# The experts' input weights read as two runs a partition, the token rows kept without a stride

## The chip, the cores and the metric

One NeuronCore of a Trainium2 chip runs the whole program in one launch. The metric is device time in microseconds (us), from one profiled execution and from runs without a profile; lower is better. All arithmetic is float32.

## The reference

Two transformer blocks in a row over 256 tokens of width 1024. The first block (two layers) mixes a convolution, a latent attention and a dilated attention. The second block has an attention over tokens and context and then a mixture of experts, cut here to what matters:

```python
logits = xt @ w_router + b_router
top_val, top_idx = lax.top_k(logits, 4)          # 4 of 32 experts a token
gates = softmax(top_val)
# for each expert e, its rows xb (tokens that chose it):
hcat = xb @ w_in[e] + b_in[e]                    # w_in[e] is 1024 x 2048
x_glu = minimum(hcat[:, :1024], 7)
x_lin = clip(hcat[:, 1024:], -7, 7)
act = x_glu * sigmoid(1.702 * x_glu) * (x_lin + 1)
y += gate * (act @ w_out[e] + b_out[e])          # w_out[e] is 1024 x 1024
```

An expert's weights are 8 MiB + 4 MiB, and all 32 experts are read once: 384 MiB of the 563 MB that the program moves.

## The kernel before

The kernel is written engine by engine. Each engine runs its own hand-ordered program, and semaphores join them: SyncE (SP) issues the DMA loads, TensorE (PE) multiplies and transposes, ScalarE (ACT) and VectorE (DVE) take results out of PSUM.

**Weights of the experts.** `ring` is an SBUF tensor of six tiles, each 128 partitions x 4096 float32 (2 MiB). An expert fills all six: tiles 0 to 3 hold w_in (256 of its 1024 rows each), tiles 4 and 5 hold w_out. `expert_tile` issues one DMA for one tile and counts it on `mlanded[j]`. Expert 0's tiles are asked for while the attention still runs. `expert(e, m)` then asks for the six tiles of the next expert, each as soon as PE has used the tile that lies there (`mused`, `lin_done`, `eout_done`); SP runs it in a loop over experts 1 to 31.

**Which row of w_in lies where.** A contraction over 1024 features is done in 8 steps of 128. Step 2j + r takes `xs[:, 2j + r, :]` (the expert's tokens, features on the partitions) and `ring[:, j, ...]`, the half r of tile j. For a given step it doesn't matter which feature sits on which partition, as long as both operands agree. Before, partition p of tile j holds rows 8p + 2j and 8p + 2j + 1, which are neighbours in HBM: one run of 16 KB a partition, with 64 KB from one partition's run to the next.

**Token rows.** After the norm the tokens lie as `h` (feature 128k + a on partition a, chunk k). PE turns them with `pe.transpose` into the PSUM bank `flip`, four chunks at a time (L830), and ACT copies each `flip` into `hTM`, tokens on the partitions (L1064). There are four such rounds, and PE waits for the copy (`flip_free`) before it turns the next four. `xs` is made per expert by `gather` (L858), which multiplies 128 columns of `hTM` at a time with a selection matrix, into `flip` and `score`; ACT copies these to `xs` (L1074). The copy of L1064 reads `flip` in a strided way, so that columns 128k to 128k + 127 of `hTM` are the features 8p + k, which is the order of the weights' rows.

**The path to the experts.** Router logits (L819), top 4 (L1297 on), the four copies, the exponential of the gates (L1068, behind the four copies in ACT's order), the gates on DVE (L1306 to L1314), their transpose (L843), the experts' output bias (L851), the first gather (L858), `xs` (L1074), and the first product of expert 0 (L869).

Of the kernel before, what the change touches and what calls it, by code (L numbers as in the profile page):

```python
# [21 lines left out]
ACT = mybir.ActivationFunctionType  # L22
AX = mybir.AxisListType

P = 128
# [3 lines left out]
DC = D // P  # L29
LAYERS = 2  # L30
EPS = 1e-6
W = 512
HALF = 64
# [186 lines left out]
def build(nc, c_in, xT, ctxT, consts, layer_params, block_params, w_in, w_uq, w_ukv, w_out_a, w_out_b, w_out_c,  # L220
          w_o, w_ada, w_qkv, w_o2, e_in, eb_in, e_out, eb_out, out, sizes=None, debug=None):
    PER = sizes or CHAINED
    with ExitStack() as ctx:
        def sb(name, shape, dt=F32):
            return ctx.enter_context(nc.sbuf_tensor(name, shape, dt))

        def sem(name):
            return ctx.enter_context(nc.semaphore(name))
# [12 lines left out]
        ring = sb("ring", [P, MRING, TILE])  # L241
# [29 lines left out]
        def take(*shape):  # L271
            n = 1
            for s in shape:
                n *= s
            v = space[:, top[0]:top[0] + n]
            top[0] += n
            if len(shape) == 2:
                return v.rearrange("p (a b) -> p a b", b=shape[1])
            if len(shape) == 3:
                return v.rearrange("p (a b c) -> p a b c", b=shape[1], c=shape[2])  # L280
            return v
# [71 lines left out]
        hTM = take(TT, D)  # L353
# [54 lines left out]
        flip = ctx.enter_context(nc.psum_tensor("flip", [P, W], F32))  # L408
# [26 lines left out]
        flip_free = sem("flip_free")  # L435
# [44 lines left out]
        mlanded = [sem(f"mlanded{i}") for i in range(MRING)]  # L480
# [35 lines left out]
        def done(l, u):  # L516

            return (l + 1) * NU + u + 1

        def split_count(l, k):  # L520

            return (l + 1) * NQ + k + 1
# [29 lines left out]
        def bdone(u):  # L552
            return (LAYERS + 1) * NU + u + 1
# [21 lines left out]
        def block_sync(sp):  # L575

            sp.wait_ge(mixed_free, MIXED0 + 1)
            sp.dma_start(bpar, block_params).then_inc(bpar_loaded, 16)
            sp.dma_start(ctx_x, ctxT).then_inc(bpar_loaded, 16)
            sources = [(w_qkv, 0, W), (w_qkv, W, 256), (w_qkv, 768, W), (w_qkv, 1280, W), (w_qkv, 1792, W)]  # L580
            sources += [(w_ada, (LAYERS * 4 + n) * W, W) for n in range(4)]
            sources += [(w_o2, 0, W), (w_o2, W, W)]
            for n, (src, a, width) in enumerate(sources):
                if n >= RING:
                    last = max(u for u, x_ in enumerate(BUNITS) if x_[1] == n - RING)
                    sp.wait_ge(unit_done, bdone(last))
                else:

                    if n < LRING:
                        sp.wait_ge(lo_done, split_count(LAYERS - 1, NQ - 1))  # L590
                    else:
                        sp.wait_ge(unit_done, done(LAYERS - 1, NU - 1))
                sp.dma_start(ring[:, n % RING, :].rearrange("p (c n) -> p c n", c=DC)[:, :, 0:width],
                             columns(src, a, width)).then_inc(landed[n % RING], 16)

            def expert_tile(we, wo, j):

                if j < 4:
                    src = we.rearrange("(p j r) n -> p j (r n)", p=P, j=4)[:, j, :]
                else:  # L600
                    src = wo.rearrange("(b p a) n -> p b (a n)", p=P, b=2)[:, j - 4, :]
                sp.dma_start(ring[:, j, :], src).then_inc(mlanded[j], 16)

            def expert(e, m):
                we = e_in[bass.ds(e, 1)].rearrange("a k n -> (a k) n")
                wo = e_out[bass.ds(e, 1)].rearrange("a k n -> (a k) n")
                for j in range(MRING):
                    if j == 3:
                        sp.wait_ge(lin_done, m)
                    elif j == 5:  # L610
                        sp.wait_ge(eout_done, m)
                    else:
                        sp.wait_ge(mused, m * 4 + (0, 1, 2, 3, 3)[j] + 1)
                    sp.sem_inc(asked, 1)
                    expert_tile(we, wo, j)

            assert (len(sources) - 2) % RING == 1
            for j in (4, 5, 3, 0, 1, 2):  # L620
                if j in (0, 3):
                    sp.wait_ge(unit_done, bdone(BQKV - 1))
                elif j in (1, 2):
                    sp.wait_ge(unit_done, bdone(NBU - 1))
                expert_tile(e_in[0], e_out[0], j)
            sp.wait_ge(mix_ready, 1)
            sp.dma_start(bout[0:NEXP, :], eb_out).then_inc(bpar_loaded, 16)
            sp.wait_ge(table_ready, 1)
            sp.dma_start(bin_sb[0:NEXP, :], eb_in).then_inc(bpar_loaded, 16)
            with sp.Fori(1, NEXP) as e:  # L630
                expert(e, e)
            sp.wait_ge(table_ready, 2)
            n_jobs = sp.value_load(jobi[0:1, MAXJOBS:MAXJOBS + 1], min_val=0, max_val=MAXJOBS)
            with sp.If(n_jobs > 0):
                with sp.Fori(0, n_jobs) as i:
                    e = sp.value_load(jobi[0:1, bass.ds(i, 1)], min_val=0, max_val=NEXP - 1)
                    expert(e, i + NEXP)
            for i in range(DC // 2):
                sp.wait_ge(final_ready, i + 1)
                sp.dma_start(out[:, 2 * i:2 * i + 2, :], h[:, 2 * i:2 * i + 2, :]).then_inc(stored, 16)  # L640
            sp.wait_ge(stored, 16 * (DC // 2))
# [341 lines left out]
        def block_scalar(act):  # L983
# [77 lines left out]
            for r in range(4):  # L1061
                t, q = r // 2, r % 2
                act.wait_ge(flipped, FLIP0 + F_TOK + r + 1)
                act.activation(hTM[:, t, :].rearrange("p (k a) -> p a k", k=DC)[:, q * HALF:(q + 1) * HALF, :],  # L1064
                               flip[:, :].rearrange("p (a k) -> p a k", k=DC), ACT.Copy).then_inc(flip_free, 1)
            act.wait_ge(gate_in, 1)
            for t in range(TT):
                ins = act.activation(gate[:, t, :], ext[:, t, 0:NEXP], ACT.Exp, bias=gsum[:, t, 0:1])  # L1068
# [376 lines left out]
        def columns(weights, a, n):  # L1445
            return weights[:, a:a + n].rearrange("(c p) n -> p c n", p=P)
# [298 lines left out]
        def _(act):  # L1745
# [214 lines left out]
            if debug != "layers":  # L1960
                block_scalar(act)
# [416 lines left out]
```

## Time and profile before

| | |
|---|---|
| median of 3 runs | 2039.31 us (2038.09 to 2044.0) |
| the profiled execution, its own time | 2037.97 us |
| its span, first to last instruction | 2036.2 us |
| mean granted TensorE clock | 0.981 |
| PE busy | 1904.2 us (94%) |
| DVE busy | 759.7 us (37%) |
| ACT busy | 546.9 us (27%) |
| DMA packets | 111407, 563.19 MB |
| in_e_in loads | 128 of 2048 KB, median 25.2 us from issue to landing |
| in_e_out loads | 64 of 2048 KB, median 22.1 us |

PE busy counts a matmul as busy while it waits in the array's pipeline, so a high share doesn't say that PE is the limit. The experts' stage is the second half of the span, from 1089 us on. The time from issue to landing of a load holds its wait behind earlier loads in the DMA queue.

### The profile page before, as it was taken

The page shows a single profiled execution, that of the slowest core. Times are in us where ns is not written, and L with a number is a line of the kernel's source. Part 1 is how long each engine was busy: PE and PEld are TensorE (multiplying, and loading weights), DVE is VectorE, ACT ScalarE, POOL GpSimd, SP SyncE. Part 2 cuts the span into 40 slices and gives each one's busy share as a digit, 9 for nine tenths or more (in the row PEclk, how much of TensorE's full clock was granted, in tenths as well). Part 3 has the DMA queues.
Part 4 walks back from the last instruction along what each step waited for, and adds up shares of the span by engine and source line. Part 5 has one row for each costly group of instructions (what it writes and reads, how often), then busy time and mean ns, then how long its engine had stood idle before and what let it go on. Part 6 is the DMA issues. An engine that isn't in the chain of part 4 may idle for free.

```text
span 2036.2 us, 26901 instructions
## 1 busy us (share of the span) xinstructions
PE 1904.2 (94%) x10970; PEld 1199.2 (59%) x10970; DVE 759.7 (37%) x1445; ACT 546.9 (27%) x922; POOL 522.6 (26%) x220
## 2 busy tenths in 40 slices
PE   7999999989999999799879999999999999999996
PEld 6779889977798899544465444333333333333433
DVE  4784643448836533734544111111111111111112
ACT  4554455445544554222411000000000000000001
POOL 5776656866755567000000000000000000000000
PEclk9999999999999999899998999999999999999999
DMA  8555333565543335421725999999999999999994
GB/s 297 200 183 176 125 125 125 172 231 176 201 150 130 120 125 189 158 75 42 287 93 208 430 428 428 430 428 429 428 428 429 428 428 429 429 429 428 428 429 193
DMA packets 111407, 563.19 MB, mean 277 GB/s; under 512 B 4768, under 2 KB 24352, under 8 KB 86464
## 3 DMA queue, kind: packets, MB, share of 16 engines
q1 hardware_dynamic: 111328, 562.09, 69.1%
q8 instruction: 56, 0.92, 0.2%
q14 instruction: 23, 0.19, 0.0%
HBM read 561.02 MB, written 1.05 MB: 276 GB/s over the span
## 4 chain that ended last, share of the span: by engine, by line
PE 57%; DMA 31%; DVE 7%; ACT 2%; issue 1%; SPq 0%; DVEq 0%; ACTq 0%
DMA ring<-in_e_in_dram 31%; PE bank L1595 14%; PE bank L1585 10%; PE score L869 9%; PE bank L695 4%; PE bank L1562 3%; PE mixed L904 2%; PE bank L802 1%; PE mixed L1679 1%; PE flip L1662 1%; DVE ring L2164 1%; PE score L1648 1%; PE flip L1620 1%; PE bank L927 1%; PE score L887 1%
## 5 line engine op out<-in xcount | busy, mean ns | idle before, releaser
L1971 POOL TENSOR_TENSOR w_lo<-ring,w_hi 128x1024 fp32r<-128x1024 f32 (+1 forms) x216 | 522.4, 2430 | 285.2 <-ACT w_hi L1873 284.6
L869 PE MATMUL score<-ring,space 128*64 128x512 f32 x2048 | 461.4, 595 | 46.2 <-DMA ring<-in_e_in_dram 45.2
L869 PEld LDWEIGHTS score<-ring,space 128*64 128x64 f32 x2048 | 142.3, 137 | 353.9 <-issue 246.2
L1873 ACT ACTIVATE w_hi<-ring 128x1024 fp32r<-128x1024 f32 (+1 forms) x216 | 226.3, 1049 | 221.5 <-PE bank L1595 122.5
L1595 PE MATMUL bank<-h_hi,w_hi 128*128 128x256 f32 x896 | 261.9, 292 | 0.0
L1595 PE MATMUL bank<-h_lo,w_hi 128*128 128x256 f32 x896 | 254.3, 284 | 0.0
L1595 PE MATMUL bank<-h_hi,w_lo 128*128 128x256 f32 x896 | 254.2, 284 | 0.0
L904 PE MATMUL mixed<-ring,space 128*64 128x512 f32 x1024 | 226.8, 595 | 0.0
L1083 ACT ACTIVATE space<-space 128x512 f32<-128x512 f32 x32 | 20.2, 631 | 718.9 <-DVE space L1375 718.9
L1375 DVE TENSOR_SCALAR space<-score 128x512 f32<-128x512 f32 x32 | 22.2, 694 | 431.7 <-PE score L869 431.7
L1595 PEld LDWEIGHTS bank<-h_hi,w_hi 128*128 128x128 f32 x896 | 172.8, 193 | 4.5 <-issue 4.4
L1595 PEld LDWEIGHTS bank<-h_lo,w_hi 128*128 128x128 f32 x896 | 172.7, 193 | 0.1
L1595 PEld LDWEIGHTS bank<-h_hi,w_lo 128*128 128x128 f32 x896 | 172.4, 192 | 0.0
L904 PEld LDWEIGHTS mixed<-ring,space 128*64 128x64 f32 x1024 | 70.7, 137 | 132.6 <-issue 130.6
L1585 PE MATMUL bank<-w_hi,h_hi 128*128 128x512 f32 (+1 forms) x320 | 131.4, 411 | 8.3 <-DVE h_lo L2027 8.3
L1388 DVE COPY space<-mixed 64x512 f32<-64x512 f32 x32 | 21.9, 685 | 295.6 <-PE mixed L904 295.6
L1585 PE MATMUL bank<-w_hi,h_lo 128*128 128x512 f32 (+1 forms) x320 | 124.9, 390 | 0.0
L1585 PE MATMUL bank<-w_lo,h_hi 128*128 128x512 f32 (+1 forms) x320 | 124.6, 389 | 0.0
L1585 PEld LDWEIGHTS bank<-w_hi,h_hi 128*128 128x128 f32 x320 | 61.0, 191 | 25.6 <-issue 12.5
L695 PE MATMUL bank<-ring,h 128*128 128x512 f32 (+1 forms) x160 | 66.6, 569 | 5.1 <-DVE h L1148 5.1
L1585 PEld LDWEIGHTS bank<-w_lo,h_hi 128*128 128x128 f32 x320 | 61.2, 191 | 11.7 <-issue 1.0
L1585 PEld LDWEIGHTS bank<-w_hi,h_lo 128*128 128x128 f32 x320 | 60.9, 190 | 12.0
(320 smaller groups left out, 2330.7 us busy)
## 6 DMA issues: line engine op xcount, KB each, us to landing
ring<-in_e_in_dram SPq DMA_DIRECT2D x128, 2048.0 KB, 25.2
ring<-in_e_out_dram SPq DMA_DIRECT2D x64, 2048.0 KB, 22.1
ring<-in_w_in_dram SPq DMA_DIRECT2D x42, 2048.0 KB, 7.8
ring<-in_w_ada_dram SPq DMA_DIRECT2D x16, 1024.0 KB, 5.4
ring<-in_w_o_dram SPq DMA_DIRECT2D x6, 2048.0 KB, 7.9
ring<-in_w_qkv_dram SPq DMA_DIRECT2D x4, 2048.0 KB, 9.9
ring<-in_w_ada_dram SPq DMA_DIRECT2D x4, 2048.0 KB, 8.0
ring<-in_w_out_a_dram SPq DMA_DIRECT2D x2, 2048.0 KB, 7.7
```

The lines of the kernel that those rows point to most:

```text
L695: ins = pe.matmul(b[:, 0:n], src[:, c, tt * P:(tt + 1) * P], w8[:, c, 0:n], start=c == 0, stop=c == DC - 1)
L802: ins = pe.matmul(b[:, i * T:(i + 1) * T], w8[:, c, m:m + P], mix[:, c, :], start=c == 0 and i == 0, stop=c == DC - 1, skip_group_check=True)
L869: ins = pe.matmul(score[HALF * blk:HALF * blk + HALF, which * W:(which + 1) * W], xs[:, 2 * j + r, HALF * hh:HALF * hh + HALF], wk[:, blk ...
L887: pe.matmul(score[HALF * blk:HALF * blk + HALF, which * W:(which + 1) * W], onehot[:, hh, :], bin_sb[:, at:at + W], start=False, stop=False)
L904: ins = pe.matmul(mixed[HALF * side:HALF * side + HALF, :], actT[:, hh, a * P + HALF * half:a * P + HALF * half + HALF], ring[:, 4 + half, ...
L1375: dve.tensor_scalar(glu[:, hh, :], score[:, 0:W], GLU_LIMIT, None, ALU.min).then_inc(glu_free, 1)
L1388: dve.tensor_copy(ys[0:HALF, hh, :], mixed[0:HALF, :])
L1562: ins = pe.matmul(b[:, i * T:(i + 1) * T], w_[:, c, m], y_[br][:, c, :], start=c == 0 and i == 0 and y_ is y_hi and w_ is hi, stop=c == 3 ...
L1585: ins = pe.matmul(b[:, 0:n], x_[:, c, t], w_[:, k % PARTS, i, 0:n], start=c == 0 and x_ is h_hi and w_ is w_hi, stop=c == DC - 1 and x_ is ...
L1595: ins = pe.matmul(b[:, half * T:(half + 1) * T], w_[:, k % PARTS, i, m:m + P], x_[:, c, :], start=c == 0 and half == 0 and x_ is h_hi and ...
L1873: act.activation(split_part(w_hi, k), raw_part(k), ACT.Copy).then_inc(hi_done, 1)
L1971: pool.tensor_tensor(split_part(w_lo, k), raw_part(k), split_part(w_hi, k), ALU.subtract).then_inc(lo_done, 1)
```

## The change

`expert_tile` reads w_in in another order: partition p of tile j now holds rows 256j + p and 256j + 128 + p, which lie 128 rows (1 MB) apart in HBM. A partition's 16 KB are two runs of 8 KB, and the tile as a whole is one contiguous 2 MiB region. Tiles 4 and 5 (w_out) are as before. Since step 2j + r now takes the features 128 (2j + r) + p, `hTM` keeps the order in which PE turns the tokens, and the copy from `flip` has no stride.

```diff
             def expert_tile(we, wo, j):
                 if j < 4:
-                    src = we.rearrange("(p j r) n -> p j (r n)", p=P, j=4)[:, j, :]
+                    src = we.rearrange("(j r p) n -> p j r n", p=P, j=4)[:, j, :, :]
+                    dst = ring[:, j, :].rearrange("p (r n) -> p r n", r=2)
                 else:
                     src = wo.rearrange("(b p a) n -> p b (a n)", p=P, b=2)[:, j - 4, :]
-                sp.dma_start(ring[:, j, :], src).then_inc(mlanded[j], 16)
+                    dst = ring[:, j, :]
+                sp.dma_start(dst, src).then_inc(mlanded[j], 16)
...
             for r in range(4):
                 t, q = r // 2, r % 2
                 act.wait_ge(flipped, FLIP0 + F_TOK + r + 1)
-                act.activation(hTM[:, t, :].rearrange("p (k a) -> p a k", k=DC)[:, q * HALF:(q + 1) * HALF, :],
-                               flip[:, :].rearrange("p (a k) -> p a k", k=DC), ACT.Copy).then_inc(flip_free, 1)
+                act.activation(hTM[:, t, q * W:(q + 1) * W], flip[:, :], ACT.Copy).then_inc(flip_free, 1)
```

SP's program, in the loop over the experts (`ISA` is the count on `asked`, `REGISTER_ALU` the loop's counters). Before:

```order
65 L602 ISA [waits mused]
66 L602 DMA ring<-in_e_in_dram 128x4096
67 L613 REGISTER_ALU
68 L602 ISA [waits mused]
69 L602 DMA ring<-in_e_in_dram 128x4096
...
76 L602 ISA [waits mused]
77 L602 DMA ring<-in_e_out_dram 128x4096
```

and now:

```order
65 L604 ISA [waits mused]
66 L604 DMA ring<-in_e_in_dram 128x2x2048
67 L615 REGISTER_ALU
68 L604 ISA [waits mused]
69 L604 DMA ring<-in_e_in_dram 128x2x2048
...
76 L604 ISA [waits mused]
77 L604 DMA ring<-in_e_out_dram 128x4096
```

Nothing moved in SP's program; the four w_in loads of an expert have a pattern of 128 x 2 runs of 2048 elements, and the w_out loads have the one that they had.

ACT's program, at the four copies of the token rows (`space` is the SBUF tensor in which `hTM`, `gate` and `xs` lie). Before:

```order
683 L1064 ACTIVATE space<-flip 128x64x8 [waits flipped] x4
684 L1068 ACT_TABLE_LOAD
685 L1068 ACTIVATE space<-space 128x32 [waits gate_in]
686 L1068 ACTIVATE space<-space 128x32
687 L1074 ACTIVATE space<-flip 128x512 [waits gathered_half]
688 L1074 ACTIVATE space<-score 128x512 [waits gathered_half]
```

and now:

```order
683 L1066 ACTIVATE space<-flip 128x512 [waits flipped] x4
684 L1069 ACT_TABLE_LOAD
685 L1069 ACTIVATE space<-space 128x32 [waits gate_in]
686 L1069 ACTIVATE space<-space 128x32
687 L1075 ACTIVATE space<-flip 128x512 [waits gathered_half]
688 L1075 ACTIVATE space<-score 128x512 [waits gathered_half]
```

The four copies stand where they stood; their pattern is now that of the later copies from `flip`. No engine has an instruction more or fewer.

## Rows read from the trace of the kernel before

**Rows 1.** The page, the span in 40 slices of 50.9 us: DMA share in tenths, GB/s.

```profile
DMA  8555333565543335421725999999999999999994
GB/s 297 200 183 176 125 125 125 172 231 176 201 150 130 120 125 189 158 75 42 287 93 208 430 428 428 430 428 429 428 428 429 428 428 429 429 429 428 428 429 193
```

**Rows 2.** The chain of waits (start us, us, what), pieces of the experts' stage.

```profile
1109.16 7.02 PE mixed L904 x32
1136.37 7.02 PE mixed L904 x32
...
1267.57 25.42 DMA ring<-in_e_in_dram
1292.99 0.04 issue
1293.04 3.68 PE score L869 x16
1296.72 0.02 issue
...
1972.39 25.43 DMA ring<-in_e_in_dram
```

**Rows 3.** Windows: us, busy us by engine, TensorE clock, DMA share, GB/s.

```profile
1122.00:1270.00 148.00, 147.31 (x735) 62.70 (x732) 28.77 (x64) 11.57 (x19) 0.00 (x0) 1.00 1.01 429
1270.00:1564.00 294.00, 274.80 (x1345) 112.83 (x1344) 50.62 (x111) 21.28 (x35) 0.00 (x0) 1.00 1.01 429
1858.00:2005.00 147.00, 137.19 (x675) 56.18 (x674) 24.26 (x50) 11.41 (x19) 0.00 (x0) 1.00 1.01 429
```

**Rows 4.** Windows of 3 and 2 us in which loads run; columns as before.

```profile
662.00:665.00 3.00, 3.00 (x27) 2.83 (x28) 0.92 (x4) 2.65 (x5) 0.00 (x0) 1.00 1.06 410
801.00:803.00 2.00, 2.00 (x19) 2.00 (x18) 0.69 (x1) 1.06 (x1) 2.00 (x1) 1.00 1.04 429
```

**Rows 5.** DMA view of 745 to 770 us, 40 slices: two loads of 4 KB rows.

```profile
GB/s 0 0 0 0 0 0 131 151 295 419 426 419 419 419 419 269 0 13 0 0 0 0 0 0 0 0 0 0 0 66 105 203 387 413 413 419 419 419 406 98
```

**Rows 6.** DMA view of 1122 to 2005 us.

```profile
DMA packets 25971, 378.33 MB, mean 428 GB/s; under 512 B 2880, under 2 KB 2880, under 8 KB 2880
q1 hardware_dynamic: 25970, 378.32, 100.6%
```

**Rows 7.** DMA view of 1304.9 to 1309.8 us, about one tile.

```profile
DMA packets 144, 2.10 MB, mean 428 GB/s; under 512 B 16, under 2 KB 16, under 8 KB 16
```

**Rows 8.** Timeline around the four copies (start us, us, engine line).

```profile
1062.72 1.03 ACT L1064 ACTIVATE space<-flip 128x512 f32<-128x512 f32 x1 [11.15 <-PE flip L830]
1063.81 0.66 PE L830 MATMUL flip<-cst,h 128*128 128x128 f32 x4 [1.12 <-ACT space L1064]
1068.64 1.04 ACT L1064 ACTIVATE space<-flip 128x512 f32<-128x512 f32 x1 [1.21 <-PE flip L830]
1069.69 1.28 ACT L1068 ACT_TABLE_LOAD   x1
1071.56 0.23 DVE L1306 TENSOR_TENSOR space<-space 128x64 f32<-128x64 f32 x1 [7.35 <-ACT space L1068]
1088.93 7.09 PE L869 MATMUL score<-ring,space 128*64 128x512 f32 x32 [0.98 <-ACT space L1074]
```

**Rows 9.** Source view of L1064 and of L1074: ns min/median/max.

```profile
L1064 ACT ACTIVATE space<-flip x4: 1030/1032/1039, 1062.7 to 1068.6; 128x512 f32<-128x512 f32 x4
L1074 ACT ACTIVATE space<-flip x17: 598/598/598, 1085.8 to 2003.5; 128x512 f32<-128x512 f32 x17
```

**Rows 10.** Windows ahead of the experts' stage; columns as before.

```profile
1067.00:1074.00 7.00, 3.85 (x18) 3.49 (x18) 1.56 (x8) 3.29 (x5) 0.00 (x0) 0.50 0.00 0
1074.00:1082.00 8.00, 7.42 (x19) 5.17 (x17) 7.24 (x26) 0.00 (x0) 0.00 (x0) 0.50 0.01 2
1082.00:1089.00 7.00, 6.01 (x35) 5.83 (x36) 6.51 (x9) 1.20 (x2) 0.00 (x0) 0.68 0.00 0
```

**Rows 11.** Window with the last of expert 0's input tiles in the queue; columns as before.

```profile
1048.00:1055.00 7.00, 0.06 (x1) 0.00 (x0) 6.11 (x11) 0.42 (x1) 0.00 (x0) 0.81 1.03 442
```

## The prediction

> **What bounds the kernel now.** I read the slices of the page first. From the 23rd slice on the DMA engines are at 9 tenths and the rate stands at 428 to 430 GB/s, while before that it changes from slice to slice [rows 1]. So the second half of the span runs at a rate that something fixes. The windows say the same more finely: from 1122 to 2005 us the DMA share is 1.01 at 429 GB/s, while PE has room from 1270 us on (274.80 busy of 294) [rows 3]. In the chain of waits the reader is to see two regimes. Early on PE's own work follows itself: one expert's output product starts at 1109.16 us and the next one's at 1136.37, so PE needs 27.2 us an expert. From 1267.57 us the chain is a DMA wait of 25.4 us, 3.68 us of PE, and the next DMA wait [rows 2]. The pieces at 1267.57 and at 1972.39 us are 24 experts apart: 704.82 / 24 = 29.37 us an expert, or 4.895 us for each of its six 2 MiB tiles. The 25.4 us are not the price of one load: they are the queue, five tiles deep. DMA needs 29.37 us an expert and PE 27.2. The first 6 experts are paid out of the tiles that were loaded ahead, and from there the end of the program is the end of the DMA stream plus a tail.
>
> Two things follow. What a tile costs on the DMA engines counts in full from the first request of the loop (expert 1's) to the last tile, also where PE seems to be the limit, since the stream never stands still in between. And what PE, ACT or DVE do inside the stage counts for nothing, as long as PE stays under 29.37. Ahead of the stage, the start of the stream counts: the first request of the loop waits until PE has used expert 0's first tile, at the end of a chain of small steps [rows 8].
>
> **Part 1: the four copies.** L1064 takes 1.032 us. The copy from the same bank, of the same 128x512 elements with no stride, takes 0.598 us (L1074) [rows 9]. The changed line has that form, so I take 0.60 for it: 4 x 0.433 = 1.73 us less. All four are on the path. PE waits 1.12 us with its next four transposes until the copy before is done, and the fourth copy stands in ACT's order ahead of the table load and the exponential, for which DVE has been waiting 7.35 us; from there the chain goes on to the first product of expert 0 at 1088.93 us [rows 8]. Next in line behind the copies are PE's counting products, which stand behind the last transposes on PE and move up with them by three copies; they were done about 1 us before DVE came to their result, so they don't take the place of the copies.
>
> Some of the 1.73 us may be given back by the clock. In this stretch PE is granted 0.50, its lower level of 1.2 GHz; PE begins to be busy without long pauses at about 1074.9 us, and the clock is back at full within the window that ends at 1089 (0.68 in the mean) [rows 10]. 0.68 over 7 us is 2.5 us at full speed. If the return comes at the same moment as before, the 1.73 us of matmuls that ran in that time at 2.4 GHz now run ahead of it at 1.2 GHz and take twice as long, so that 0.87 us of the gain is left. I take the middle of 0.87 and 1.73, **-1.3 us**.
>
> **Part 2: the loads.** Each w_in tile was 128 runs of 16 KB, 8 an engine, and is now 256 runs of 8 KB, 16 an engine. A tile's window holds 144 packets, 128 of 16 KB and 16 small ones that close the load [rows 7]. The bytes are the same, so the question is what 8 more packets cost an engine. 31 experts pass the loop (expert 0's tiles come before it and lie landed for some 30 us before PE asks for them, which covers theirs): 31 x 4 x 8 = 992 more packets on each engine, one after another in a stream that never pauses.
>
> The trace of before has no saturated stream of 8 KB packets, so I bound the price from the other sizes.
> - 2 KB packets: with loads of 2 KB rows running, the rate is 410 GB/s (the first of [rows 4]). A tile would take 2.097 MB / 410 = 5.115 us, 0.220 us more than 4.895, with 64 packets an engine in place of 8. 0.220 / 56 = 3.9 ns a packet.
> - 4 KB packets: six slices in the middle of a load run at 419 (once 426), 420 in the mean [rows 5]. A tile would take 4.993 us, 0.098 more for 24 more packets: 4.1 ns a packet.
> - 8 KB packets: in the 2 us of a 1 MB load of such rows the rate is 429 (the second of [rows 4]), that of the 16 KB stream. By this the price is nothing. But the window is short against the 16 packets of 0.3 us that it cuts at each end, so it is a weak row; it is the lower end.
> - By the packets' own durations instead of the rate: 3 us x 16 engines x 1.06 over 1.23 MB / 2048 B = 600 packets is 84.8 ns for one of 2 KB [rows 4]. One of 16 KB is at most 883 us x 16 x 1.006 / 23,090 = 615.5 ns (25,970 less 2880 small ones) [rows 6]. (8 x 84.8 - 615.5) / 7 = 9.0 ns a packet. This is the upper end. It counts the overlap of a packet with the next one as cost, which the share of 1.06 shows to be there (over 1.00 can't be throughput), so I trust it less than the rates.
>
> I take 4.0 ns, since two sizes agree on it and 8 KB lies between one of them and the 16 KB that I measure from: 992 x 4.0 = **+4.0 us**, with 0 and 992 x 9.0 = +8.9 us as ends. An expert becomes 29.37 + 4 x 8 x 0.004 = 29.50 us. PE stays 2.3 us under it, so no part of it is hidden. SP issues as many DMAs as before, each about 20 us ahead of its turn in the queue; a longer issue would be covered by that queue, and only if the queue were empty would it show, once a tile.
>
> The Trainium skill weighs in here with another view of the limit: *DMA: Bandwidth & Descriptors*, section "Where 436 GB/s comes from", holds that for loads from HBM the HBM side binds, at about 358 GB/s a core, and not the port side (435). If that were the limit, a packet's overhead in the engine would be hidden behind HBM, part 2 would be nothing and the sum would be -1.3 us. The trace disagrees with 358: the stream holds 428 (the page itself allows more when the other core is idle).
>
> **Sum.** -1.3 + 4.0 = +2.7 us on the profiled execution's own 2037.97 us (1.8 us more than its span of 2036.2) gives 2040.7. The median of the runs shown, 2039.31, is 1.3 us above the profiled execution; on it the forecast is **2042.0 us**, +0.13%.
>
> **Rivals.** Differences under 0.3%, 6.1 us, are about what a measurement of this kernel can't tell from no change.
> 1. Slower: a packet costs what its duration says, 9.0 ns. Then +8.9 - 1.3 = +7.6, 2046.9 us. It decides from (6.1 + 1.3) / 992 = 7.5 ns a packet. For it speaks that durations are what the engines themselves record; against it that two rates at two sizes give half of it. A variant is that the jump of 1 MB between the two halves of a partition costs HBM something; loads of 2 KB rows jump at every packet and yet fit 4 ns. Chance 0.16.
> 2. The packets are free, as the 429 row would have it: -1.3 us, 2038.0 us. Chance 0.13.
> 3. Faster: the old pattern is what holds the stream at 428, since one partition's run is 64 KB from the next, and the contiguous tile runs quicker. The best rate that a longer window shows is 442 GB/s, over 7 us in which the last tiles of expert 0 come in [rows 11]. A w_in tile at 442 takes 4.745 us, 0.150 less: 124 x 0.150 = 18.6 us, and with part 1 the time is 2019.4 us. Against it: that 442 is itself from tiles of the old pattern; and w_out tiles are contiguous already, yet a third of the stream being such tiles leaves no trace, the rate standing at 428 to 430 in every slice [rows 1] and at 428 in the window of a single tile [rows 7]. It would decide from 6.1 - 1.3 = 4.8 us, 0.039 us a tile. Chance 0.05. A rule stands beside it: the Trainium skill's *DMA: Bandwidth & Descriptors*, "Latency and other measured facts", warns of row pitches at large powers of two in HBM, with measured losses from 512 KiB on, and advises to lay tiles out contiguously. By that rule the old 64 KB pitch is the suspect one and the change repairs it; no row here shows a loss at 64 KB.
>
> The forecast itself (a packet at 1 to 7 ns) has 0.62, and 0.04 is for something unseen, such as a clock that returns later ahead of the stage or at the tail.
>
> **How the numbers follow.** Within 0.3% are the forecast and rival 2, and half of the unseen: 0.77. Slower is rival 1 with a little of the unseen: 0.17. Faster: 0.06. The ends of the sum are -1.7 + 0 and -0.9 + 8.9, which on the median is 2037.6 to 2047.3. The runs of before spread over 6 us, with two of three within 1.2, so I widen the lower end by 1.6 and hold the upper: 2036 to 2047.5.
>
> **What the changed profile would show.** Right: packets rise by 128 x 128 = 16384 to some 127,790, with the count under 8 KB unchanged. An expert's period in the chain is 29.50 us (29.37 if the packets are free, 29.66 at 9 ns), and the stream's rate about 426.5 GB/s at a share above 1.00. The copies (now L1066) take 0.60 us and the first product of expert 0 starts at 1087.2 to 1088.1 us. Clock around it: still 0.50 from about 1066 us. Wrong: a period below 29.3 would be rival 3; a DMA share below 1 in the stage would mean that another part, such as issue by SP or the making of descriptors, limits the stream; and PE waiting elsewhere than on in_e_in tiles would mean that the change moved the wait.

## The result, and the profile after

The changed kernel takes 2046.56 us in the median of 14 runs (2044.14 to 2051.76); the kernel before, on the same chips, 2038.14 (2036.64 to 2044.0). The ratio is 1.0039, interval 1.003 to 1.0048: slower by 0.4%, some 8 us. The profiled executions differ by 7.1 us in their spans (2036.2 and 2043.3).

The page of the changed kernel: its DMA share and rate in 40 slices, the packets, and the queue's share of 16 engines.

```profile
DMA  8555333565544235411726999999999999999994
GB/s 296 201 183 174 125 124 124 178 232 178 193 145 146 103 136 194 161 53 42 288 90 256 425 423 424 425 422 425 424 425 423 424 425 423 423 425 425 422 425 193
DMA packets 127791, 563.19 MB, mean 276 GB/s; under 512 B 4768, under 2 KB 24352, under 8 KB 86464
q1 hardware_dynamic: 127712, 562.09, 69.5%
```

The same bytes come in 127,791 packets, 16,384 more. In the experts' stage the rate is 422 to 425 GB/s where it was 428 to 430 [rows 1], and the DMA share is as full as before (1.01 in the window below). The first half of the span is much as it was.

The chain of waits of the changed kernel, from the first product of expert 0 to the last wait for a w_in tile:

```profile
1086.69 7.09 PE score L871 x32
...
1266.92 25.73 DMA ring<-in_e_in_dram
...
1979.11 25.75 DMA ring<-in_e_in_dram
2004.86 0.04 issue
```

1266.92 and 1979.11 are 24 experts apart: 29.675 us an expert, where it was 29.37 [rows 2]. Laid out by the chains, the 7.1 us are: the first product of expert 0 2.24 us earlier (1086.69 for 1088.93, [rows 8]); from there to the landing of the last w_in tile 918.17 us for 908.89 (the wait of 25.43 us from 1972.39 ends at 1997.82), so 9.28 more; and from that landing to the end 38.44 for 38.38. The sum is +7.1.

Windows of the changed kernel, columns as in [rows 3], one of the stage and one ahead of it:

```profile
1270.00:1564.00 294.00, 271.78 (x1327) 110.12 (x1326) 48.43 (x104) 21.26 (x35) 0.00 (x0) 1.00 1.01 424
```

```profile
1082.00:1089.00 7.00, 5.99 (x39) 4.40 (x40) 5.66 (x10) 1.20 (x2) 0.00 (x0) 0.90 0.00 0
```

In the stage PE has more room than before (271.78 busy of 294, for 274.80), so DMA is still the slower one. Ahead of it the granted clock of 1082 to 1089 us is 0.90 in the mean, for 0.68 [rows 10]. The copies, source view:

```profile
L1066 ACT ACTIVATE space<-flip x4: 598/598/599, 1063.1 to 1067.6; 128x512 f32<-128x512 f32 x4
```

598 ns each, for 1032 [rows 9].

### The profile page after: what moved, and what is told of

It reads as the page before. It is cut to its first block, busy times and chain, and to the rows that moved or that the text cites. A ratio compares the mean times of both kernels' runs of the same rounds, so it can differ in the third digit from the quotient of the medians.

```text
span 2043.3 us, 26901 instructions
## 1 busy us (share of the span) xinstructions
PE 1904.1 (93%) x10970; PEld 1198.6 (59%) x10970; DVE 759.8 (37%) x1445; ACT 545.1 (27%) x922; POOL 522.4 (26%) x220
## 2 busy tenths in 40 slices
DMA packets 127791, 563.19 MB, mean 276 GB/s; under 512 B 4768, under 2 KB 24352, under 8 KB 86464
## 3 DMA queue, kind: packets, MB, share of 16 engines
HBM read 561.02 MB, written 1.05 MB: 275 GB/s over the span
## 4 chain that ended last, share of the span: by engine, by line
PE 56%; DMA 33%; DVE 7%; ACT 2%; issue 1%; SPq 0%; DVEq 0%; ACTq 0%
DMA ring<-in_e_in_dram 33%; PE bank L1596 14%; PE bank L1586 10%; PE score L871 9%; PE bank L697 4%; PE bank L1563 3%; PE mixed L906 2%; PE bank L804 1%; PE mixed L1680 1%; PE flip L1663 1%; DVE ring L2165 1%; PE score L1649 1%; PE flip L1621 1%; PE bank L929 1%; PE score L1693 1%
```

## The experiments

Two theories for the 0.307 us that an expert costs more. **A**: the count of packets, 32 more an engine and expert, each at 9.6 ns. **B**: only 4 ns of that is the count's, as the prediction took it, and the rest is the tile's new place in HBM, a contiguous region read with jumps of 1 MB. A has its 9.6 ns from this result, so it takes other kernels to test it. A period below is the distance of two waits in the chain, divided by the experts between them. "Before" beside a time is the kernel before on the same chip.

### The count or the place

**Runs of 8 KB in the old 64 KB block** (e1_runs8_near).

```diff
-src = we.rearrange("(j r p) n -> p j r n", p=P, j=4)[:, j, :, :]
+src = we.rearrange("(p r j) n -> p j r n", p=P, j=4)[:, j, :, :]
...
```

The copies of the token rows, left out here, are strided again, to fit this order of rows.

> The w_in tiles keep the old place in HBM (each partition its own block of 64 KB), but a partition's 16 KB are two runs of 8 KB, 32 KB apart (rows 8p + j and 8p + 4 + j). Theory A (the count of packets alone costs, 9.6 ns for each more on an engine): the period of an expert in the chain is 29.67 us as in the changed kernel. Theory B (only some 4 ns a packet are the count's, and the rest comes from the new place: a contiguous tile read with jumps of 1 MB): 29.50 us. The token copies are here 8 strided ones of 128x256, so the first product of expert 0 may start later than in both kernels, by either theory.

Its chain:

```profile
1267.87 25.73 DMA ring<-in_e_in_dram
...
1979.95 25.75 DMA ring<-in_e_in_dram
```

712.08 / 24 = 29.67 us. The place is the old one and the period the new one: theory B fell. One run took 2047.28 us (before 2038.77).

**A contiguous tile in runs of 16 KB** (e2_contig16, and again as e11_contig16_again).

```diff
-src = we.rearrange("(p j r) n -> p j (r n)", p=P, j=4)[:, j, :]
+src = we.rearrange("(j p r) n -> p j (r n)", p=P, j=4)[:, j, :]
...
-hTM[:, t, (4 * q + i) * P:(4 * q + i + 1) * P],
+hTM[:, t, (2 * q + i // 2) * 2 * P + i % 2:(2 * q + i // 2 + 1) * 2 * P:2],
```

The copies are the ones without a stride.

> The w_in tiles are contiguous 2 MiB regions as in the changed kernel, but a partition holds two neighbouring rows, one run of 16 KB (rows 256j + 2p and 256j + 2p + 1). The copies of the token rows have no stride; the gather reads every second column as PE's stationary operand. Theory A: 29.37 us an expert, as before the change, and with the cheaper copies some 2 us less than before, 2036. Theory B: between 29.37 and 29.67, about 29.5, since the tile's place is the new one. If a stationary operand with a stride is slow to load, PE's gathers get longer; PE has 2.2 us of room an expert, and two gathers of 16 products ahead of the stage lie on the path.

> The kernel with contiguous tiles in 16 KB runs and copies without a stride again, beside the two above: 29.37 us an expert and a ratio of 0.9988, 2.5 us under the kernel before, as far as five rounds can tell.

The chain, and the gather in the source view (ns min/median/max):

```profile
1292.98 25.43 DMA ring<-in_e_in_dram
...
1968.38 25.42 DMA ring<-in_e_in_dram
```

```profile
L858 PEld LDWEIGHTS flip<-space x272: 192/197/331, 1078.4 to 1999.2; 128*128 128x128 f32 x136
```

675.40 / 23 = 29.37 us, the period of before, from the contiguous place: A once more, from the other side. Loading every second column as stationary operand (the one loaded into PE ahead of a product) takes 197 ns in the median, against 191 in both kernels. The times are 2034.98 us (before 2038.77; ratio 0.999, 0.9979 to 1.0) and 2038.22 (before 2037.87; 0.9996, 0.9987 to 1.0005). One of the 12 runs behind the second time took 4524.81 us, and the ratio leaves it out; the median without it is 2037.9, and why it was so long is not known. So this layout has the changed kernel's copies without its packets, is 0.4 to 0.5% faster than the changed kernel by the two ratios, and against the kernel before can't be told from no change. The profiled span of e2_contig16, 2030.7 us, is 5.5 us under that of before, but only 2.5 us of that lie between L823 and expert 0's first product (25.0 us for 27.5); another 1.5 are the sums of the last norm at the end of the program (L980), with 3.73 us for 5.26, in which the next kernel and the changed one differ as well. Most of the rest lies ahead of L823.

**w_out in runs of 8 KB too** (e4_wout8).

```diff
-src = wo.rearrange("(b p a) n -> p b (a n)", p=P, b=2)[:, j - 4, :]
-dst = ring[:, j, :]
+src = wo.rearrange("(b s p a) n -> p b s (a n)", p=P, b=2, s=2)[:, j - 4, :, :]
+dst = ring[:, j, :].rearrange("p (s n) -> p s n", s=2)
...
-lin[:, hh, a::4]
+lin[:, hh, 256 * (a // 2) + a % 2:256 * (a // 2 + 1):2]
```

> The changed kernel with its w_out tiles too in two runs of 8 KB (rows 128 pairs apart), so 16 more packets an engine and expert. Theory A: 29.67 + 16 x 0.0096 = 29.83 us an expert, 4.8 us more in all than the changed kernel. Theory B (place of w_in): the w_out tiles add only 16 x 0.004 = 0.07 us, 29.74. If something else in the alternation of the two packet sizes costs the extra, the period stays at 29.67 or falls.

```profile
1267.18 25.87 DMA ring<-in_e_in_dram
...
1983.17 25.89 DMA ring<-in_e_in_dram
```

715.99 / 24 = 29.83 us, as A had it. The one time, 2047.69 us (before 2038.77), is less than the 4.8 us over the changed kernel that a longer stream should give, but the chain shows the whole of it: from expert 0's first product (1085.91 us) to the last landing of a w_in tile (1983.17 + 25.89 = 2009.06) it is 923.15 us, 5.0 more than the changed kernel's 918.17. What is missing is in the tail, where the 16 products that sum up the last norm are quicker; here those of the changed kernel first, then this kernel's:

```profile
2029.04 5.33 PE score L982 x16
```

```profile
2033.24 3.73 PE score L982 x16
```

Around them the granted clock is 0.69 in the mean in the changed kernel (2029.0 to 2034.4 us) and 1.00 in this one (2033.2 to 2037.0). In the kernel before they take 5.26 us.

### What a packet costs, from 2 KB to 32 KB

**Runs of 4 KB and of 2 KB** (e6_runs4, e7_runs2), the changed kernel with each w_in row in pieces:

```diff
-src = we.rearrange("(j r p) n -> p j r n", p=P, j=4)[:, j, :, :]
-dst = ring[:, j, :].rearrange("p (r n) -> p r n", r=2)
+src = we.rearrange("(j r p) (w n) -> p j w r n", p=P, j=4, w=2)[:, j, :, :, :]
+dst = ring[:, j, :].rearrange("p (w r n) -> p w r n", w=2, r=2)
...
```

This is the 4 KB kernel; the 2 KB kernel has `w=4`. The products, left out here, take the pieces from where they now lie in the tile.

> The changed kernel with each w_in row in two halves, so a tile is 512 packets of 4 KB, 32 an engine. Theory A in the form that the queued stream of the four kernels so far gives it (a packet lasts 9.3 ns plus its bytes at 27.2 bytes a ns, so 159.8 ns): 5.12 us a tile, 30.26 us an expert. By the prediction's 4 ns a packet, from loads that run alone: 4.99 us a tile, 29.76 us an expert.

> The same with rows in four quarters: a tile is 1024 packets of 2 KB, 64 an engine. Fixed price in the queued stream: 84.5 ns a packet, 5.41 us a tile, 31.4 us an expert, and the stream of w_in tiles at 387 GB/s. By the prediction's 4 ns: 5.12 us a tile, 30.26 us an expert (410 GB/s). If PE's slack matters too, nothing of it shows, since DMA stays the slower one.

The chain of the 4 KB kernel, then of the 2 KB kernel (24 and 20 experts apart):

```profile
1230.21 26.25 DMA ring<-in_e_in_dram
...
1956.59 26.30 DMA ring<-in_e_in_dram
```

```profile
1297.65 27.16 DMA ring<-in_e_in_dram
...
1927.04 27.18 DMA ring<-in_e_in_dram
```

726.38 / 24 = 30.27 us and 629.39 / 20 = 31.47 us, both where the fixed price of the queued stream puts them and far from the prediction's 4 ns (29.76 and 30.26). One run each: 2062.31 and 2099.09 us (before 2038.15).

**Longer runs: pairs of tiles in one load** (e8_pairs32), from the kernel before:

```diff
-for j in range(MRING):
+for j in (1, 3, 4, 5):
...
+src = we.rearrange("(p t r) n -> p t (r n)", p=P, t=2)[:, j // 2, :]
+dst = ring[:, j - 1:j + 1, :].rearrange("p s n -> p (s n)")
...
```

Load 1 brings tiles 0 and 1, load 3 brings tiles 2 and 3, and PE waits for the pair ahead of its first tile.

> The other way round: the kernel before with tiles 0 and 1, and 2 and 3, loaded by one DMA each, so a partition's run is 32 KB and an engine gets 8 packets in place of 16 for 4 MB. The copies are those of the kernel before. Fixed price of 9.3 ns: 16 packets fewer an engine and expert, and two closing ones fewer: 29.37 - 0.15 - 0.01 = 29.21 us an expert, 5 us less in all. A rival: a pair can be asked for only when both its tiles are used, so the queue gets shallower; if the DMA share falls below 1, the gain is lost. Another: packets over 16 KB are cut, and nothing changes.

The chain in the stage, then at its end:

```profile
1215.60 21.85 DMA ring<-in_e_in_dram
...
1975.24 21.84 DMA ring<-in_e_in_dram
1997.08 0.04 issue
1997.12 7.11 PE score L869 x32
```

759.64 / 26 = 29.22 us: the stream got quicker by 0.15 us an expert, as forecast, and neither rival in its named form came true. But the time is 2039.25 us (before 2038.15; ratio 1.0001, 0.9989 to 1.0012). The chain shows where the 4.7 us of 31 experts went. The loop's first load goes out at 1096.90 us, when PE has used expert 0's second tile, for 1092.83 before (its first product started 0.64 later here, so 3.4 us are the pair's). And behind the last landing PE has the products of two tiles to do, 7.11 us, for 3.68 [rows 2]: 3.4 us more.

**Only tiles 1 and 2 as a pair**, with the old copies (e9_pair12) and, from contiguous regions, with the new ones (e10_pair12_copies; its gathers read every second or every fourth column):

```diff
-for j in range(MRING):
+for j in (0, 2, 3, 4, 5):
...
```

Load 2 brings tiles 1 and 2, and PE waits for it ahead of tile 1.

> The kernel before with tiles 1 and 2 alone loaded by one DMA, in runs of 32 KB; tile 0, which lets the stream start, and tile 3, behind which PE's tail stands, stay single. Fixed price of 9.3 ns: 8 packets fewer an engine and expert and one closing one: 29.37 - 0.08 = 29.29 us an expert, 2.5 us less in all than before, 0.12%. If the 5 us that the pairs (0,1) and (2,3) saved were lost to the later start and the longer tail, as their chains say, nothing is lost here; if they were lost to something in the stream itself, such as 32 KB packets, the time is again that of before.

> The same 32 KB run for tiles 1 and 2, and 16 KB for 0 and 3, but from contiguous regions (as in the run with contiguous tiles and 16 KB runs), with copies without a stride and gathers that read every second or every fourth column. 29.29 us an expert and a first product of expert 0 some 2.5 us earlier after the logits: 5 us less than before, ratio 0.9975. Rival: a stationary operand with a stride of 16 bytes loads at 335 ns like the one of 32 bytes; with half of the gather's products on it PE needs about 1.1 us more an expert, still under 29.3, but the gathers ahead of the stage lose about 1 us.

Both missed. The end of the stage in the chain of e9_pair12, with the same 16 products one expert earlier on top:

```profile
1963.87 3.65 PE score L871 x16
...
1972.93 20.20 DMA ring<-in_e_in_dram
1993.13 0.04 issue
1993.17 5.35 PE score L871 x16
1998.52 1.72 PE score L889 x8
2000.24 6.89 PE score L871 x32
```

and the gathers of e10_pair12_copies:

```profile
L865 PEld LDWEIGHTS flip<-space x272: 193/312/332, 1079.0 to 2006.1; 128*128 128x128 f32 x136
L865 PE MATMUL flip<-space x272: 280/397/581, 1079.0 to 2006.2; 128*128 128x128 f32 x136
```

The period is 29.29 us in both (in e10, 1268.08 to 1971.09 over 24 experts), as forecast. What I had overlooked is that a pair is of use only when its second tile is in, and can be asked for only when its second place is free. It costs at both ends.

At the end, PE has three tiles and the bias to work off behind the landing of the pair: in e10_pair12_copies 3.65, 1.72 and 6.87 us, 12.2 in a row behind 1991.34 us. Before, it was one tile's 3.68 us, behind a landing that comes one tile (4.9 us) later in the stream. That is 3.7 us more.

At the start, the first request of the loop is at 1092.45 us in e9_pair12 and the next one, for the pair, only at 1101.04, when PE has used expert 0's tile 2. Before, the request for tile 1 stood by itself and went out at 1096.26. The DMA engines stand still in between; first e9_pair12, then before, columns as in [rows 3]:

```profile
1099.00:1101.50 2.50, 2.50 (x16) 0.82 (x14) 0.00 (x0) 0.00 (x0) 0.00 (x0) 1.00 0.00 0
```

```profile
1098.00:1102.00 4.00, 4.00 (x22) 1.48 (x20) 0.00 (x0) 0.00 (x0) 0.00 (x0) 1.00 1.05 451
```

This hole is some 3.1 us: from expert 0's first product to the landing of the last pair it is 904.6 us in e9 and 904.7 in e10, where 904.0 is the same distance of before to the last tile 2 (908.89 less one tile) and the longer runs should have saved 2.4.

In e9_pair12 a third item comes in. Its 16 products behind the last landing took 5.35 us, against 3.65 for the same ones an expert earlier and in e10, and the granted clock from 1993 to 1998.5 us is 0.69 in the mean, where it was 1.00 from 1963.8 to 1967.6. Ahead of these products PE had stood idle for 2.05 us, but a wait of 2.04 us two experts earlier was followed by 3.65 us, so the wait alone doesn't explain it. That is 1.7 us of this trace.

The sum from the first product to the end of the w_in products is 3.7 + 3.1 - 2.4 = +4.4 us, and e10 has +4.4 (917.0 for 912.6); with the 1.7 it is +6.1, and e9 has +6.0. The times are 2043.89 us for e9 (before 2037.87; ratio 1.0029, 1.0017 to 1.0041) and, with the new copies, 2041.26 for e10 (1.0019, 1.001 to 1.0028); there a stationary operand of every fourth column loads in 312 to 332 ns, as the rival had it.

### Part 1 alone, and part 2 alone

**The copies alone** (e3_copies_only), from the kernel before:

```diff
-act.activation(hTM[:, t, :].rearrange("p (k a) -> p a k", k=DC)[:, q * HALF:(q + 1) * HALF, :],
-               flip[:, :].rearrange("p (a k) -> p a k", k=DC), ACT.Copy)
+act.activation(hTM[:, t, q * W:(q + 1) * W], flip[:, :], ACT.Copy)
...
-hTM[:, t, (4 * q + i) * P:(4 * q + i + 1) * P],
+hTM[:, t, 4 * q + i::DC],
```

> The loads are those of the kernel before, and the four copies have no stride, as in the changed kernel; the gather takes every eighth column of the token rows as PE's stationary operand instead. Part 1 of the change alone. Both theories: 29.37 us an expert; the copies take 0.60 us and the first product of expert 0 starts 1.7 to 2.6 us earlier than before (the changed kernel's was 2.2 earlier), so that the time is 0.1% under the kernel before, 2036. Rival: the stationary operand with a stride of 32 bytes loads slower, and the gather ahead of the first product eats the gain.

Source view of the gather, and a window of the stage:

```profile
L858 PEld LDWEIGHTS flip<-space x272: 312/337/338, 1081.3 to 2006.8; 128*128 128x128 f32 x136
```

```profile
1270.00:1564.00 294.00, 294.00 (x1366) 135.91 (x1364) 50.47 (x110) 20.73 (x35) 0.00 (x0) 1.00 1.01 429
```

The rival won. The stationary operand with a stride of 32 bytes takes 337 ns to load, for 191, and PE is busy for all of the stage's window (294.00 of 294). Even so the stream is still what paces the stage: two waits in the chain that are two experts apart, at 1916.80 and 1975.53 us, give 29.37 us an expert. Ahead of the stage the gather takes 7.85 us for 5.91, which eats the copies' gain: from the small products ahead of the transposes (L823) to expert 0's first product it is 27.5 us as before. Behind the last landing the gathers stand on the path too:

```profile
1975.53 24.04 DMA ring<-in_e_in_dram
...
2003.27 4.02 PE flip L858 x16
...
2007.76 3.79 PE score L858 x16
```

From that landing (1999.57 us) to the end it is 43.2 us, for 38.4 before: 4.8 of the 6.6 us between the two profiles. The gathers make 3.5 of them (the last output product starts 11.98 us behind the landing, for 8.45), the sums of the last norm 1.4 (6.62 for 5.26). The time is 2044.44 us (before 2038.77; ratio 1.003, 1.0019 to 1.0041). It moved the work and doesn't measure part 1 by itself; the next run does, by difference.

**The loads alone** (e5_loads_only): the changed kernel with the old copies. It leaves out that the two operands agree on which feature lies where, so its output is not the reference's; the work and its order are the same.

> The changed kernel's loads with the strided copies of the kernel before, so the product takes features of the weights against other features of the tokens and the output is another one; the work and its order are those of the kernels. If the parts add up: 29.67 us an expert, the first product of expert 0 some 2 us later than in the changed kernel, and the time 2 us above it, 9 to 10 us above the kernel before (ratio 1.0047). If the loads alone cost less than that, part 1 has no gain of its own.

Its chain, start us, us, what:

```profile
1270.55 25.76 DMA ring<-in_e_in_dram
...
1982.84 25.76 DMA ring<-in_e_in_dram
```

29.68 us an expert. From L825 (the L823 of before) at 1062.83 us to expert 0's first product at 1090.31 it is 27.5 us; in the changed kernel 24.9 (1061.81 to 1086.69). The time is 2050.88 us (before 2038.15; ratio 1.0057, 1.0037 to 1.0077), 0.18% (3.7 us) over the changed kernel's ratio, which agrees with 2.6 us within the two intervals.

### One load at a time

The last question was why the rates of [rows 4, 5] had given 4 ns. **2 KB runs with one load in flight** (e12_runs2_alone), from e7_runs2:

```diff
 sp.sem_inc(asked, 1)
+sp.wait_ge(mlanded[(j + 5) % 6], m * 16 + (16 if j else 0))
+sp.sem_inc(asked, 1)
 expert_tile(we, wo, j)
```

The new wait is for the landing of the tile before.

> The kernel with w_in in 2 KB runs, and SP asks for a tile only when the tile before it has landed, so one load runs at a time. The time grows by hundreds of us and isn't the point. The point is the pace of 2 KB packets in the middle of a w_in load: if a queue of several loads is what slows a packet, it is 410 GB/s as in the loads of the first block that run alone (80 ns a packet). If it stays at 386 to 388 GB/s (84.5 ns), something else in the experts' loads is slower than in the first block's, and the queue isn't it.

Windows of 3 us inside w_in loads, first of e7_runs2 (queued), then of this kernel, columns as in [rows 3]:

```profile
1316.00:1319.00 3.00, 3.00 (x18) 0.98 (x14) 0.00 (x0) 0.00 (x0) 0.00 (x0) 1.00 1.05 388
1325.00:1328.00 3.00, 3.00 (x16) 1.00 (x16) 0.00 (x0) 0.00 (x0) 0.00 (x0) 1.00 1.05 385
```

```profile
1507.50:1510.50 3.00, 2.24 (x8) 0.49 (x4) 0.00 (x0) 0.00 (x0) 0.00 (x0) 0.75 1.05 409
1516.50:1519.50 3.00, 3.00 (x16) 0.84 (x12) 0.00 (x0) 0.00 (x0) 0.00 (x0) 1.00 1.05 408
```

The same tiles, packets and addresses run at 385 to 388 GB/s with others queued behind them and at 408 to 409 alone. With 16 engines, a packet of 2048 B then takes 16 x 2048 B over the rate: 84.8 and 80.2 ns, 4.6 ns more in the queue. The second windows of the two have PE as busy (3.00 of 3), so it isn't how busy PE is that differs. The program as a whole takes 2685.99 us so (before 2038.33).

## Why the prediction was right or wrong

**The direction and the range held, the size didn't.** The forecast was +2.7 us; measured are 7.1 us between the profiles and 8.4 between the medians (ratio 1.0039). The time of 2046.56 us lies near the upper end of the range, and the case that happened is the first rival, which had a chance of 0.16: 2046.9 us from 9.0 ns a packet. That the time lies inside the range at all has some luck in it. The range was laid on the 2039.31 us of three runs; the 14 runs of the kernel before have a median of 2038.14, and on that the range's upper end of 2047.5 would have been 2046.3, under what was measured. And two errors pulled against each other: the packets cost 5.5 us more than forecast, part 1 gained 1.3 us more.

**What bounds the kernel** was read rightly. In every run whose loads were queued, the period followed the DMA work of a tile, and the span followed the period, with what the start and the end of the stream add.

**The step that failed is the choice of 4.0 ns for a packet** (the term of +4.0 us). With the measured 9.6 ns it is 992 x 9.6 = +9.5 us, and with the 2.6 us that part 1 gained the sum is +6.9, against 7.1 between the profiles. Against the period of before (29.3675 us), the runs give:

| kernel | packets more an engine and expert | period, us | ns a packet |
|---|---|---|---|
| changed | 32 | 29.675 | 9.6 |
| w_out too | 48 | 29.833 | 9.7 |
| 4 KB | 96 | 30.266 | 9.4 |
| 2 KB | 224 | 31.47 | 9.4 |
| 32 KB pairs | -16 (and 2 closing ones) | 29.217 | 9.4, the closing ones in it |
| 32 KB, one pair | -8 (and 1 closing one) | 29.292 | 9.4, the closing one in it |

So the price is one figure, 9.4 to 9.7 ns, over runs from 2 to 32 KB. The upper end that I had from the durations (9.0) was nearly it. I trusted the rates more, because two sizes agreed on 4 ns. They agreed since both carried the same error. The small packets of [rows 4, 5] stood in loads that ran alone, the 16 KB ones of [rows 3, 6] in a queue, and a packet in the queue lasts some 4 to 5 ns longer: 4.6 ns by the test with 2 KB packets, and for 4 KB packets 160 ns in the queue (406 to 412 GB/s in windows of e6_runs4) against 156 in the lone loads of [rows 5], for which there is no test of their own. The difference of the two kinds undercounts the price of a packet by about that. A share of 1.06 over 1.01 was no argument against the durations either: with 2 KB packets in the queue the share is 1.05 too, and there the price is 9.4.

**The 429 GB/s of the 8 KB row** (the second of [rows 4]) was called a weak row and was one; it too is a lone load.

**Part 1** was right in kind, and its size was off the other way: 598 ns a copy, as taken from L1074, but 2.6 us gained (27.5 to 24.9 from the same product on) for my 1.3, and for 1.73 at the most. 1.86 us of it are there by the start of the products with the experts' output bias (13.38 and 11.52 us behind L823 and L825), the rest comes behind it. I had feared that the clock would come back at the same moment and so take some of the gain. It came back earlier by more than the copies' gain: the window mean of 0.90 for 0.68 says so, and the first gather took 5.18 us for 5.91. In the traces with strided copies (the kernel before, e1, e5, e8, e9) the stretch is 27.5 us, in those with the new copies and at most every second column (changed, e2, e4, e6, e7, e11) 24.9 to 25.0. The new copies alone don't bring this. e3_copies_only has them too, and the bias products start as early in it (11.52 us behind L823), but its clock came back as late as before. The windows of one microsecond in which it comes back, in the kernel before, the changed one and e3_copies_only:

```profile
1086.00:1087.00 1.00, 1.00 (x9) 1.00 (x8) 1.00 (x1) 0.39 (x1) 0.00 (x0) 0.76 0.00 0
```

```profile
1083.00:1084.00 1.00, 1.00 (x9) 1.00 (x9) 1.00 (x1) 0.07 (x1) 0.00 (x0) 0.80 0.00 0
```

```profile
1087.00:1088.00 1.00, 1.00 (x6) 1.00 (x5) 0.62 (x4) 0.00 (x0) 0.00 (x0) 0.67 0.00 0
```

With 0.50 until then and 1.00 from then on, that is 25.0, 21.6 and 25.0 us behind L823 (L825). So about 0.7 us of part 1's 2.6 us hang on when the clock returns, and in e3, whose gather differs, it didn't return early. How the chip picks the moment isn't settled here.

**The cover of expert 0's tiles, the unchanged issue on SP and the unmoved wait of PE** were right: the period is DMA's own, and PE waits for in_e_in tiles as before.

**Rival 3**, that the old place slows the stream, was wrong: 16 KB runs go at 29.37 us an expert from 64 KB blocks and from contiguous tiles alike, and 8 KB runs at 29.67 from both. So nothing falls to the pitch rule of the Trainium skill (*DMA: Bandwidth & Descriptors*, "Latency and other measured facts") at 64 KB, which is under the pitches that it has losses for.

The Trainium skill's *DMA: Bandwidth & Descriptors*, section "Why small descriptors are slow", gives a packet a fixed overhead of about 3 cycles inside the engine, which at the 850 MHz that the page states for the fabric would be an estimated 3.5 ns. The measured 9.4 to 9.7 ns is over twice that.

## What to carry to other kernels

Where a queued stream of loads is the limit, count its packets. Each run of contiguous bytes had a fixed price on its DMA engine, here 9.5 ns, which is 1.5% of a 16 KB packet and 11% of a 2 KB one. A rearrangement that halves the runs pays it however tidy the region looks, and the runs could be kept long here with the cheap copies all the same (two neighbouring rows a partition, and every second column in the product). Take the price from packets in the same kind of queue as those that it is for, and don't set a lone load's rate against a queue's. Loads merged to save packets are worth it only if what starts and what ends the stream keeps its fine grain: here the first requests and the work behind the last landing gave back all that the longer runs saved, or more. And where a stage waits for a stream, look at the work at its two ends: in e3_copies_only the longer gathers inside the stage left the period at 29.37 us, while those ahead of it took back the copies' gain and those behind it added 3.5 us.

## What was unexpected

- A packet takes 4 to 5 ns less when its load is alone in the queue: 409 GB/s for 386 with 2 KB packets, from the same tiles. Why is open.
- The price of a packet doesn't depend on where it reads: runs 32 KB apart and 1 MB apart, in blocks of 64 KB or in contiguous tiles, have the same period within 0.01 us.
- Loading a stationary operand of 128x128 float32 takes 191 ns with no stride, 197 from every second column, 312 to 332 from every fourth and 337 from every eighth (e2, e10, e3).
- The same 16 products that sum up the last norm took 3.73 us in six traces (e2, e4, e6, e7, e10, e11) 5.26 to 5.42 in six others (before, changed, e1, e5, e8, e9) and 6.62 in e3. In the two looked at above, the granted clock differed with it. The spans of single profiled executions can differ by 1.6 us for that alone.
